# A hybrid attention / HGRN2 / conv-FFN layer on one core: the input projection streams high and low activation halves in one 512-column matmul, and VectorE adds the two halves when a PSUM bank is read

## The reference, cut to what matters

```
h   = rms_norm(x, attn_norm)                  # x: 256 tokens x 2048
p   = h @ w_in                                # 2048 x 5376
aq, ak, av, hq, hf, hi, hg = split(p, ...)    # 1024, 128, 128, 1024, 1024, 1024, 1024
attn_out = sliding_window_attention(aq, ak, av, q_norm, k_norm, sinks)   # RMS of q, k; softmax with sink
hg_out   = hgrn2(silu(hq), lower_bound + (1 - lower_bound) * sigmoid(hf), hi, silu(hg), ...)
x   = x + concat(attn_out, hg_out) @ w_out
h   = rms_norm(x, ffn_norm)
x   = x + (silu(a) * b) @ w_down,  [a, b] = causal conv3(h @ w_up)
```

## Time and profile before

| | |
|---|---|
| median of 3 runs | 1142.5 us (1142.47 to 1142.5) |
| the profiled execution's own time | 1142.53 us |
| its span, first to last instruction | 1140.7 us |
| PE busy | 1126.0 us (99%) |
| DVE busy | 789.5 us (69%) |
| ACT busy | 590.0 us (52%) |
| DMA, mean | 179 GB/s |

### The profile page before, as it was taken

One profiled execution on the slowest core, in us unless ns is written; L12 is line 12 of the kernel. 1 busy time (PEld: TensorE's weight loads), 2 busy tenths in 40 slices (PEclk: granted clock), 3 DMA queues, 4 the chain that ended last, 5 costly groups with the idle time before them and its releaser, 6 DMA issues.

```text
span 1140.7 us, 19577 instructions
## 1 busy us (share of the span) xinstructions
PE 1126.0 (99%) x6956; PEld 986.0 (86%) x6956; DVE 789.5 (69%) x1200; ACT 590.0 (52%) x840; POOL 5.9 (1%) x33
## 2 busy tenths in 40 slices
PE   6999999999999999999999999999999999999998
PEld 5989999999988888888888888888888888888886
DVE  6878868687765568877787877778787644444443
ACT  7577655556554465555554555555455433333332
POOL 2000000000000000000000000000000000000000
PEclk9999999999999999999999999999999999999999
DMA  7644555555556656665556566665656565656562
GB/s 227 187 130 129 160 157 165 153 160 164 159 157 189 182 162 205 192 190 188 186 189 194 184 190 191 188 187 188 195 183 190 190 190 185 205 187 208 187 207 75
DMA packets 171996, 204.16 MB, mean 179 GB/s; under 512 B 6437, under 2 KB 139958, under 8 KB 171702
## 3 DMA queue, kind: packets, MB, share of 16 engines
q1 hardware_dynamic: 170854, 201.57, 57.6%
q10 hardware_dynamic: 1104, 2.10, 0.5%
HBM read 201.54 MB, written 2.10 MB: 179 GB/s over the span
## 4 chain that ended last, share of the span: by engine, by line
PE 97%; DVE 1%; ACT 1%; DMA 0%; issue 0%; ACTq 0%
PE bank L1176 28%; PE bank L1177 14%; PE bank L1207 10%; PE bank L1208 10%; PE bank L1206 10%; PE bank L1190 7%; PE bank L1192 7%; PE bank L1193 7%; PE bank L1144 1%; PE bank L1341 1%; DVE hs L721 0%; DMA xt<-in_x_dram 0%; ACT squares L427 0%; PE bank L1294 0%; PE bank L1381 0%; PE bank L1346 0%
## 5 line engine op out<-in xcount | busy, mean ns | idle before, releaser
L701 DVE TENSOR_TENSOR w_lo<-raw,w_hi 128x1024 fp32r<-128x1024 f32 x380 | 463.6, 1223 | 298.9 <-ACT w_hi L401 298.2
L401 ACT CAST w_hi<-raw 128x1024 fp32r<-128x1024 f32 x380 | 398.5, 1051 | 463.6 <-PE bank L1208 189.2
L1176 PE MATMUL bank<-hs,w_hi 128*128 128x512 f32 x1408 | 488.9, 394 | 0.2 <-DVE hs L721 0.2
L1177 PE MATMUL bank<-hs,w_lo 128*128 128x256 f32 x1408 | 390.2, 277 | 0.0
L1176 PEld LDWEIGHTS bank<-hs,w_hi 128*128 128x128 f32 x1408 | 264.0, 188 | 61.8 <-DVE hs L721 0.5
L1177 PEld LDWEIGHTS bank<-hs,w_lo 128*128 128x128 f32 x1408 | 264.4, 188 | 0.1
L1190 PE MATMUL bank<-hs,w_hi 128*128 128x256 f32 x672 | 194.9, 290 | 0.5 <-DVE w_lo L701 0.5
L1192 PE MATMUL bank<-hs,w_hi 128*128 128x256 f32 x672 | 190.0, 283 | 0.0
L1193 PE MATMUL bank<-hs,w_lo 128*128 128x256 f32 x672 | 190.0, 283 | 0.0
L1206 PE MATMUL bank<-w_hi,gated 128*128 128x512 f32 x352 | 139.2, 396 | 0.0
L1207 PE MATMUL bank<-w_lo,gated 128*128 128x512 f32 x352 | 139.2, 396 | 0.0
(11 more groups left out here) (185 smaller groups left out, 726.4 us busy)
## 6 DMA issues: line engine op xcount, KB each, us to landing
raw<-in_w_ffn_up_dram SPq DMA_DIRECT2D x176, 512.0 KB, 3.6
raw<-in_w_ffn_down_dram SPq DMA_DIRECT2D x88, 512.0 KB, 4.5
raw<-in_w_in_dram SPq DMA_DIRECT2D x84, 512.0 KB, 3.8
raw<-in_w_out_dram SPq DMA_DIRECT2D x32, 512.0 KB, 4.2
xt<-in_x_dram SPq DMA_DIRECT2D x2, 1024.0 KB, 6.0
out_dram<-xt ACTq DMA_DIRECT2D x3, 512.0 KB, 7.2
out_dram<-xt ACTq DMA_DIRECT2D x2, 256.0 KB, 2.5
rows<-in_ffn_conv_w_dram SPq DMA_DIRECT2D x3, 44.0 KB
```

Of the source, the lines that this page charges most:

```text
L401: act.copy(w_hi[:, i, :], raw[:, i, :]).then_inc(units_hi, 1)
L701: dve.tensor_tensor(w_lo[:, i, :], raw[:, i, :], w_hi[:, i, :].bitcast(F32), ALU.subtract)\
L1176: pe.matmul(banks[b][:, :], w_hi[:, i, c], x_k, start=(i == 0 and k == 0), stop=False)
L1177: last = pe.matmul(banks[b][:, 0:SEQ], w_lo[:, i, c], x_k[:, 0:SEQ], start=False, stop=(i == RING - 1 and k == 3))
```

## The change

`unit_w_in` now does what `unit_channels` does: for each block b and row tile k one matmul of 512 columns and one of 256, with the blocks in two different banks. Block 0 of a unit is done for all four row tiles before block 1. The banks are named anew: in the attention part each quad has its two banks from a table (`W_IN_BANKS`), later quads q and g use the pair of banks 0 and 1, and f and i the pair 6 and 7. DVE adds the halves of a completed quad into SBUF: in the attention part by two tensor_reduce of 512 columns each (`sum_halves`), later by one of 1024 (`sum_pair`), each placed just ahead of the last `make_lo` of a slot. The ACT copies of the i and v banks go, since the sums lie in SBUF already; squares, sigmoids and products read the sums.

```
-            def unit_w_in(quad, i, dst):
+            def unit_w_in(quad, i, banks, summed):
                 pe.wait_ge(units_split, quad * RING + i + 1 + RING)
-                for k in range(4):
-                    x_hi, x_lo = hs[:, 4 * i + k, 0:SEQ], hs[:, 4 * i + k, SEQ:2 * SEQ]
-                    for b in range(2):
+                for b in range(2):
+                    if i == 0 and summed[b] is not None:
+                        pe.wait_ge(w_in_summed, summed[b])
+                    for k in range(4):
                         c = slice(k * GC + b * P, k * GC + (b + 1) * P)
-                        o = dst[:, b * SEQ:(b + 1) * SEQ]
-                        pe.matmul(o, w_hi[:, i, c], x_hi, start=(i == 0 and k == 0 and b == 0), stop=False,
-                                  skip_group_check=True)
-                        pe.matmul(o, w_hi[:, i, c], x_lo, start=False, stop=False, skip_group_check=True)
-                        last = pe.matmul(o, w_lo[:, i, c], x_hi, start=False,
-                                         stop=(i == RING - 1 and k == 3), skip_group_check=True)
+                        x_k = hs[:, 4 * i + k, :]
+                        pe.matmul(banks[b][:, :], w_hi[:, i, c], x_k, start=(i == 0 and k == 0), stop=False)
+                        last = pe.matmul(banks[b][:, 0:SEQ], w_lo[:, i, c], x_k[:, 0:SEQ], start=False,
+                                         stop=(i == RING - 1 and k == 3))
+                    if b == 0 and i == RING - 1:
+                        last.then_inc(first_half_done, 1)
                 last.then_inc(units_used, 1)
...
+        W_IN_BANKS = [(0, 1), (6, 7), (1, 6), (0, 1), (7, 0), (1, 7), (0, 1)]
+            def sum_halves(quad, b, dst):
+                if b == 0:
+                    dve.wait_ge(first_half_done, quad + 1)
+                else:
+                    dve.wait_ge(units_used, (quad + 2) * RING)
+                src = w_in_banks[quad][b]
+                dve.tensor_reduce(dst, src.rearrange("p (h t) -> p t h", h=2), AX, ALU.add).then_inc(w_in_summed, 1)
+            def sum_pair(quad, src, dst):
+                dve.wait_ge(units_used, (quad + 2) * RING)
+                dve.tensor_reduce(dst, src[:, :, :].rearrange("p b (h t) -> p b t h", h=2), AX, ALU.add)\
+                    .then_inc(w_in_summed, 2)
...
-                act.wait_ge(units_used, (quad + 1) * RING)
-                act.activation(SQ[:, :], bank[(quad - 1) % 2][:, :], ACT.Square).then_inc(att_squared, 1)
+                act.wait_ge(w_in_summed, 2 * quad)
+                act.activation(SQ[:, :], QN[:, :, :].rearrange("p a t -> p (a t)"), ACT.Square)\
+                    .then_inc(att_squared, 1)
...
                 scale_p(g, 1)
+                for b in range(2):
+                    sum_halves(quad, b, QN[:, b, :] if g < Q_GROUPS - 1 else SG[:, b * SEQ:(b + 1) * SEQ])
                 make_lo(quad + 1, 3)
...
             def g_slot(j, quad):
-                pe.wait_ge(silu_q, j + 1)
-                unit_w_in(quad, 0, bank_g)
+                unit_in_pair(quad, 0, pair_g)
                 pe.wait_ge(o_normed, j + FREE)
-                pe.wait_ge(i_copied, j + 1)
+                pe.wait_ge(w_in_summed, quad * 2)
```

More of the change, by code:

```diff
@@ L205, in hybrid_layer @@
         gated = sb_at(place, "gated", [P, KT_FF, 2 * SEQ], F32R)
-        bank = [ctx.enter_context(nc.psum_tensor(f"bank{i}", [P, 512], F32)) for i in range(8)]
+        bank_pair = [ctx.enter_context(nc.psum_tensor(f"bank_pair{i}", [P, 2, 512], F32)) for i in range(4)]
+        bank = [bank_pair[i // 2][:, i % 2, :] for i in range(8)]
         loaded = [sem(f"loaded{i}") for i in range(RING)]
@@ L275, in pair_of, with sums_before @@
             return bank[b], bank[b + 1]
-        bank_s, bank_p, bank_o_att, bank_m = bank[2:4], bank[4:6], bank[6], bank[7]
-        bank_f = bank_i = bank[1]
-        bank_q = bank_g = bank[0]
+        bank_s, bank_p, bank_o_att, bank_m = bank[2:4], bank[4:6], bank[6], bank[2]
+        W_IN_BANKS = [(0, 1), (6, 7), (1, 6), (0, 1), (7, 0), (1, 7), (0, 1)]
+        w_in_banks = [(bank[a], bank[b]) for a, b in W_IN_BANKS]
+        def sums_before(quad, b):
+            same = [2 * q + half + 1 for q in range(quad) for half in range(2)
+                    if W_IN_BANKS[q][half] == W_IN_BANKS[quad][b]]
+            return same[-1] if same else None
+        pair_f = pair_i = bank_pair[3]
+        pair_q = pair_g = bank_pair[0]
         bank_scores = [bank[2:4], bank[4:6]]
-        bank_o, bank_mean, bank_v = bank[6], bank[7], bank[7]
+        bank_o, bank_mean, bank_v = bank[4], bank[5], bank[4]
         CROSS, WITHIN = slice(P, 2 * P), 2 * P
@@ L768, in _ @@
             dve.wait_ge(params_made, 1)
-            for i in range(1, RING):
+            for i in range(1, RING - 1):
                 make_lo(1, i)
+            sum_halves(0, 0, QN[:, 0, :])
+            sum_halves(0, 1, FE[:, 1, :])
+            make_lo(1, RING - 1)
             dve.wait_ge(pool_done, 1)
@@ L824, in _ @@
                                     QN[g * HEAD_DIM:(g + 1) * HEAD_DIM, 0, :]).then_inc(kz_made, 1)
-            for i in range(1, RING):
+            for i in range(1, RING - 1):
                 make_lo(2, i)
             dve.wait_ge(kz_made, 6)
+            for b in range(2):
+                sum_halves(1, b, QN[:, b, :])
+            make_lo(2, RING - 1)
             def bias_and_max(g, h):
@@ L1019, in g_slot, with f_slot_of_next @@
                 gather_scores(j, 1)
+                sum_pair(quad, pair_g, GE[:, :, :])
                 make_lo(quad + 1, 3)
-            def f_slot_of_next(j, quad):
+            def f_slot_of_next(j, quad, last=False):
                 clamp(j * 3 + 2)
@@ L1035, in f_slot_of_next @@
                 make_lo(quad + 1, 2)
+                if not last:
+                    sum_pair(quad, pair_f, SG[:, :].rearrange("p (a t) -> p a t", a=2))
                 make_lo(quad + 1, 3)
```

110 lines of the change are left out of this document (56 added, 54 removed).

## The result

The changed kernel takes 1176.6 us (median of 4 runs, 1176.2 to 1177.5), the kernel before 1142.5 us beside it: ratio 1.030, 95% interval 1.028 to 1.032. It is **34.1 us slower**; the forecast was 1166 us, and the upper end of the range, 1176, was just missed.

What follows compares the result with a forecast made beforehand. The prediction took PE's stream to bound the input projection, with DVE late at two places. Pair 0's +13.3 us (attention's lateness included), +10.2 for later pairs and -0.3 made +23.2 on 1142.5: 1166 us, range 1151 to 1176.

Steps and rivals of the forecast that it cites:

- the two places that were named: PE waits for DVE's sums behind scale_p in each attention slot, and for the sum into IE before its transposes.
- Attention +9.2: Quad 6's first unit ends 9.2 us later: 2.8 at the first mean plus 1.6 in each of four slots.
- pair 0's transposes +13.3: The first head pair's transposes of IE, waiting for the sum behind QB, come 13.3 us later than before.
- a period 56.0: Time between the IE transposes of successive head pairs: 34.4 + 21.6 = 56.0 us against 52.58, +3.4 each.
- the forecast proper: Both places stall and the clock keeps its full rate: 1166 us, own range 1158 to 1171, chance 0.62.
- the case in which the clock falls: Rival: PE's clock halves behind the four IE waits, 2 us each, giving 1174 us; chance 0.15.
- the forecast's 23.2: Total lateness at the end of the input projection: 13.3 + 10.2 - 0.3 = +23.2 us.
- The wide stream: One 512-column matmul replaces two of 256: 84 units x 0.11 = -9.2 us, if PE is never held up.
- The new waits: PE waiting for DVE, about 32 us in all, of which four of 5 us ahead of the IE transposes.
- The waits are hidden: Rival: DVE catches up ahead of its late sums, leaving only the faster matmul stream: 1133 us; chance 0.07.
- one place only: Rival: only attention stalls, 1145 us, or only the head pairs stall, 1154 us; chance 0.12.
- The wide stream is no faster: Rival: the 512-column matmuls save no time here, 1175 us if every unit counted; chance 0.04.

Runs made afterwards that it cites:

- the kernel with all fillers: The changed kernel plus unused matmuls: 19 in each wait ahead of the IE transposes, 12 in PE's first attention wait; 1167.0 us.
- The two kernels in which one place alone stalls: The changed kernel with only the sum into IE moved earlier (1155.5 us), or only the attention sums moved earlier (1166.3 us).
- both places eased: The changed kernel with both the attention sums and the sum into IE moved earlier in DVE's order; 1143.8 us.

## Why the prediction was right or wrong

**Which way, and where.** Right: slower, PE waiting in the two places that were named, for the two kinds of sums, because of their place in DVE's order. Moving them shows it (10.3 and 21.1 us back).

**The sizes of the late sums.** Right, as far as the clock keeps. Attention +9.2 against 9.8 measured without the clock's fall, pair 0's transposes +13.3 against 13.7, a period 56.0 against 56.0, the whole 1166 against 1166.3 in the profiled execution of the kernel with all fillers, and 1167.0 at its median. The bank table did decide the attention slots: PE waits for the first sum (L744), and the third slot lost 18.39 - 16.78 = 1.6, as summed up. With all fillers, so without the clock, the last three slots lost 1.5 to 1.7 each, and the first 2.0: the means at its two ends start at 47.38 and 64.49 there, at 44.42 and 59.55 in the kernel before. That is most of the 0.6 us between 9.2 and 9.8. The period's exact hit has some luck in it. In the kernel with all fillers the stretch from the transposes to ACT's release took 34.7 us (34.4 put) and the one from there to the end of the sum 21.3 (21.6 put), so two errors of 0.3 cancel. One reading of the prediction was too strong: from 78.87 to 92.94 DVE does not work quite back to back, it waits 0.93 us for ACT ahead of the `make_lo` at 80.55. The chain is still DVE's, as the 1.6 us per slot show.

**The step that failed** is the clock: the forecast proper let the waits of 5 us cost only their length, and the case in which the clock falls had 0.15. It falls in all four pairs and once in attention. The price of it was nearly right for a pair (2 us put, 58.2 - 56.0 = 2.2 measured in the first), but the rival left out the attention part, where the first wait of 2.9 us is followed by 3.4 us of half clock: 11.35 - 9.8 = 1.6 us. Four pairs at about 2.1 and this one are 10 us, and with the forecast's 23.2 they make 33 of the 34.1 us. The profiled executions of the change and of the kernel with all fillers say the same: 1176.3 against 1166.3. The evidence was at hand in the earlier trace rows, half pace behind a wait of 8.95 us, and in the rule of the Trainium skill that the rival cites; I held a shorter wait to be open and then weighed it as unlikely, which no row supported.

**The wide stream** was mis-sized: -9.2 put, -6.1 measured alone. The sum still came out since PE's stream hardly counts while it waits: taking it back costs 0.6 us in the change, with shorter half-clock stretches set against it. The new waits are accordingly a little shorter than put: 28.7 instead of about 32 us, and 4.7 instead of 5 in a pair.

**Rivals.** "The waits are hidden" is refuted (4.7 us in each pair), "one place only" too. The two kernels in which one place alone stalls took 1155.5 and 1166.3 us, where that rival had 1145 and 1154. The clock's fall is part of both differences, and another part is that some 1.1 us of waits for DVE stay in each pair when the sum into `IE` is early: with both places eased the time is still 1143.8 us and not 1133. "The wide stream is no faster" is refuted by 6.1 us in the kernel before.

## What to carry to other kernels

When a reader moves from one engine to another, look at where its result stands in the new engine's fixed order and not at that engine's idle share: DVE had 13 us free per pair, and one line in the wrong place cost 5 us a pair, 2.1 of them by the clock. A new wait of TensorE can cost more than its length, because the clock may halve behind it: here always at 3.3 to 4.7 us, sometimes at 2.2 to 3.0. Price it at half of the work that PE then does at the lower level, 1.5 to 2.2 us for each wait here, and give that case a real chance. A gain in the pace of a stream is worth something only while that stream is the path, so remove the waits first and then measure the gain.

## What the runs showed of the hardware that was not expected

- Waits of PE of 4.7 us were each followed by work at half clock until 4.6 to 4.8 us after the transposes began, in a stretch of 6.8 us. Those of 3.3 and 4.0 us brought a stretch of 3.4. One of 2.92 us brought none in one place while one of 2.91 us elsewhere did, and of the waits of 2.2 us at one place of the attention part one in five traces did. So the length of the wait alone does not decide at 2 to 3 us.
- More work made the kernel faster: 76 unused matmuls in the waits (19 in each of four) took 9.3 us off.
- The start distance of the same 512 + 256 pair is 0.346 us in some stretches and 0.353 in others at a granted clock of 1.00, without a wait in the trace; the cause is open.
